# Moving the second half of a cross-attention value projection from the attention to behind the expert queries, with merge gates in quarter slots

## The reference, cut to what matters

```
h = rmsnorm(x)
ya = moba_attention(...)              # 8 heads
yb = nsa_attention(...)               # 8 heads: compressed, selected and window branch
g = sigmoid(h @ w_merge_gate + b_merge)          # 2 x 1024 columns
merged = g[:, :, 0] * (ya @ w_up_a) + g[:, :, 1] * (yb @ w_up_b)
x = x + merged @ w_out
x = x + peer_ffn(rmsnorm(x), ...)     # expert queries, key scores, top 16, experts u and v
for layer in (0, 1):
    ...
    kv = mem @ xa_wkv[layer]          # keys and values of the memory: do not depend on x
    x = layer_norm(alpha * x + cross_attend(x, kv, ...))
    ...
```

## Time and profile before

| | |
|---|---|
| median of 3 runs | 1773.57 us (1771.17 to 1774.9) |
| profiled execution, its own time from first to last instruction | 1771.5 us |
| its mean granted TensorE clock | 0.995 |
| TensorE busy | 1735.8 us, 98% |
| VectorE busy | 1119.2 us, 63% |
| ScalarE busy | 240.8 us, 14% |
| GpSimd busy | 301.4 us, 17% |
| DMA moved | 439.62 MB, mean 248 GB/s |

### The profile page before, as it was taken

One profiled execution on the slowest core, in us unless ns is written; L12 is line 12 of the kernel. 1 busy time (PEld: TensorE's weight loads), 2 busy tenths in 40 slices (PEclk: granted clock), 3 DMA queues, 4 the chain that ended last, 5 costly groups with the idle time before them and its releaser, 6 DMA issues.

```text
span 1771.5 us, 29553 instructions
## 1 busy us (share of the span) xinstructions
PE 1735.8 (98%) x11793; PEld 1482.8 (84%) x11793; DVE 1119.2 (63%) x2415; ACT 240.8 (14%) x599; POOL 301.4 (17%) x282
## 2 busy tenths in 40 slices
PE   8999999999999899999999999999999999999996
PEld 7898576986999899999999868699955978699942
DVE  4752432898657888799533533279974763379964
ACT  1014520110414111000000011111100001011100
POOL 0010000145433444444422200000000000000000
PEclk9999999999999999999999999999999999999998
DMA  7534234499999999999999844365554435354551
GB/s 276 190 122 164 72 119 143 155 337 372 414 416 416 405 407 398 373 412 415 415 417 418 344 202 160 126 223 172 171 173 166 167 121 191 117 170 167 170 182 50
DMA packets 76609, 439.62 MB, mean 248 GB/s; under 512 B 8566, under 2 KB 8656, under 8 KB 37840
## 3 DMA queue, kind: packets, MB, share of 16 engines
q1 hardware_dynamic: 42624, 305.15, 46.4%
q0 software_dynamic: 32592, 125.92, 18.3%
q10 hardware_dynamic: 1280, 6.95, 1.0%
HBM read 432.67 MB, written 5.24 MB: 247 GB/s over the span
## 4 chain that ended last, share of the span: by engine, by line
PE 81%; DMA 9%; DVE 8%; issue 1%; ACT 1%; POOL 0%; SPq 0%; POOLq 0%; DVEq 0%
PE ps L1139 16%; PE ps L921 14%; PE ps L540 10%; DMA arena<-u_rows,sparse_pairs 7%; PE ps L584 7%; PE ps L913 7%; PE ps L1177 4%; PE ps L623 3%; PE ps L498 3%; DVE arena L1912 2%; PE ps L776 2%; PE ps L823 2%; PE ps L789 1%; PE ps L934 1%; PE ps L1008 1%
## 5 line engine op out<-in xcount | busy, mean ns | idle before, releaser
L913 PE MATMUL ps<-xT,ring 128*128 128x150 f32 x2048 | 268.4, 293 | 0.0
L921 PE MATMUL ps<-arena,ring 128*128 128x150 f32 (+1 forms) x2048 | 266.3, 292 | 0.8 <-DMA ring<-stream 0.8
L913 PEld LDWEIGHTS ps<-xT,ring 128*128 128x128 f32 x2048 | 264.4, 191 | 0.1
L921 PEld LDWEIGHTS ps<-arena,ring 128*128 128x128 f32 x2048 | 262.3, 190 | 1.5 <-issue 1.5
L540 PE MATMUL ps<-ring,arena 128*128 128x512 f32 x416 | 181.4, 592 | 0.4 <-ACT arena L1487 0.4
L2033 DVE SCALAR_TENSOR_TENSOR arena<-arena,sparse_dots 128x1024 f32<-128x1024 f32 x105 | 134.7, 1283 | 73.4 <-DMA arena<-v_rows,sparse_pairs 68.2
L2501 POOL DMA_INDIRECT arena<-v_rows,sparse_pairs x107 | 132.8, 1241 | 224.9 <-DVE arena L2033 180.4
L1912 DVE CUSTOM_DVE_ANT_0 arena<-arena 128x1024 f32<-128x1024 f32 x107 | 127.9, 1223 | 66.9 <-DMA arena<-u_rows,sparse_pairs 66.3
L2501 POOL DMA_INDIRECT arena<-u_rows,sparse_pairs x107 | 132.4, 1238 | 167.9 <-DVE sparse_dots L1912 143.7
L2464 POOL TENSOR_SCALAR stat<-stat 128x1 f32<-128x1 f32 (+2 forms) x23 | 4.4, 190 | 913.8 <-DVE stat L2205 705.7
L540 PEld LDWEIGHTS ps<-ring,arena 128*128 128x128 f32 x416 | 78.0, 190 | 93.0 <-issue 92.3
(11 more groups left out here) (341 smaller groups left out, 2244.2 us busy)
## 6 DMA issues: line engine op xcount, KB each, us to landing
ring<-stream SPq DMA_DIRECT2D x288, 1024.0 KB, 7.5
arena<-second_params POOLq DMA_DIRECT2D x6, 1024.0 KB, 5.2
arena<-kv_scratch POOLq DMA_DIRECT2D x2, 2048.0 KB, 14.2
kv_scratch<-arena ACTq DMA_DIRECT2D x2, 1024.0 KB, 10.7
arena<-held_params ACTq DMA_DIRECT2D x1, 2048.0 KB, 16.5
arena<-u_rows,sparse_pairs POOLq DMA_INDIRECT x107, 13.7
arena<-v_rows,sparse_pairs POOLq DMA_INDIRECT x107, 11.2
arena<-second_params POOLq DMA_DIRECT2D x1, 1536.0 KB, 6.5
```

The lines of the kernel that those rows point to most:

```text
L913: ins = pe.matmul(ps[:, o % 2, 0:DENSE], w[:, (o % 2) * D + k * P:(o % 2) * D + (k + 1) * P], xT[:, k, 0:DENSE], start=(k == 0), stop=(k = ...
L921: ins = pe.matmul(ps[:, 4 + k // 2, c:c + DENSE], w[:, (o % 2) * D + k * P:(o % 2) * D + (k + 1) * P], H[:, n, :], start=False, stop=last, ...
```

## The change

In the attention, the merge gates are spread over all 16 units (4 products of 256 columns a unit, a quarter of a slot; a gate after units 3, 7, 11 and 15), and the section `v0` leaves it. `v0` now stands behind `peer_q` and ahead of `k1`, in the same form as `v1` (`memory_values`). Its stage in SBUF moves to the place of the upper expert queries, its spill moves from POOL's queue to ScalarE's, and ScalarE's wait for the spills stands after 8 turns of the expert loop and not after 12. The first memory spill keeps its place. The waits for the old spill on ScalarE, VectorE and POOL go away.

```
-            ("v0", 4), ("merge", 4), ("w_out", 4), ("peer_q", 8), ("k1", 4), ("v1", 4),
+            ("merge", 4), ("w_out", 4), ("peer_q", 8), ("v0", 4), ("k1", 4), ("v1", 4),
...
+        v0_stage = pqT[:, 8:16].rearrange("p j t -> p (j t)").rearrange("p (i n) -> p i n", i=TT)
...
             def fill(n):
 
-                if n < 8:
-                    s, t = n // 2, n % 2
-                    if t == 0:
-                        if s:
-                            pe.wait_ge(mgate_ready, 4 + s)
-                        fill_slots["gate"] = slot("mgate_b", s)
...
-                half, i, kh = (n - 8) // 4, n // 2 % 2, n % 2
...
-                for k in range(4):
-                    ins = pe.matmul(ps[:, 6, :], memT[:, 4 * kh + k, i * P:(i + 1) * P],
-                                    fill_slots[kh][:, k * 512:(k + 1) * 512],
-                                    start=(kh == 0 and k == 0), stop=(kh == 1 and k == 3))
...
+                s, t, kh = n // 4, n // 2 % 2, n % 2
+                if t == 0 and kh == 0:
+                    if s:
+                        pe.wait_ge(mgate_ready, 4 + s)
+                    fill_slots["gate"] = slot("mgate_b", s)
+                w = fill_slots["gate"]
+                for k in range(4 * kh, 4 * kh + 4):
+                    ins = pe.matmul(ps[:, 6, t * T:(t + 1) * T], w[:, k * 2 * P + t * P:k * 2 * P + (t + 1) * P],
+                                    xT[:, k, :], start=(k == 0), stop=(k == KT - 1))
+                if t == 1 and kh == 1:
                     ins.then_inc(slot_done, 1)
...
+            memory_values("v0", K0_FIRST)
             for c in range(4):
-                if c >= 2:
-                    pe.wait_ge(xkv_ready, KV_EARLY + c - 1)
+                pe.wait_ge(xkv_ready, KV_EARLY + c - 1)
                 feature_major(slot("k1", c), 4 + c % 2, memT).then_inc(slot_done, 1)
...
             def fill_copy(n):
 
-                if n % 2 == 0:
-                    return
-                if n < 8:
-                    merge_gate(4 + n // 2, START["mgate_b"] + n // 2 + 1, 6)
-                    return
...
-                act.copy(v0_stage[:, i, half * 512:(half + 1) * 512], ps[:, 6, :]).then_inc(xkv_ready, 1)
+                if n % 4 == 3:
+                    merge_gate(4 + n // 4, START["mgate_b"] + n // 4 + 1, 6)
...
-            act.wait_ge(kv_spilled, 32)
...
+            values_out("v0", v0_stage, 0)
+            act.wait_ge(xkv_ready, KV_EARLY)
+            act.dma_start(kv_scratch[0][:, KT * T:], v0_stage.rearrange("p i n -> p (i n)")).then_inc(v0_spilled, 16)
+            gate_exponentials(0)
...
-            at = 12
+            at = 8
...
+            act.wait_ge(v0_spilled, 16)
             act.wait_ge(kv1_spilled, 32)
...
-            dve.wait_ge(kv_spilled, 32)
...
-            pool.dma_start(kv_scratch[0][:, HALF_KV:], kv_stage[:, HALF_KV:]).then_inc(kv_spilled, 16)
```

More of the change, by code:

```diff
@@ L877, in _, with memory_values @@
             key_scores(PH + 3)
+            def memory_values(section, before):
+                for half in range(2):
+                    slots = [slot(section, 2 * half + kh) for kh in range(2)]
+                    for i in range(TT):
+                        if half or before > KV_EARLY:
+                            pe.wait_ge(xkv_ready, before + 2 * half + i - 1)
+                        for kh in range(2):
+                            for k in range(4):
+                                ins = pe.matmul(ps[:, 4 + i, :], memT[:, 4 * kh + k, i * P:(i + 1) * P],
+                                                slots[kh][:, k * 512:(k + 1) * 512],
+                                                start=(kh == 0 and k == 0), stop=(kh == 1 and k == 3))
+                            if i == 1:
+                                ins.then_inc(slot_done, 1)
+                        if i == 0:
+                            ins.then_inc(v_psum, 1)
+            memory_values("v0", K0_FIRST)
             for c in range(4):
[L879 to L880 removed]
+                pe.wait_ge(xkv_ready, KV_EARLY + c - 1)
                 feature_major(slot("k1", c), 4 + c % 2, memT).then_inc(slot_done, 1)
[L882 to L894 removed]
+            memory_values("v1", KV_EARLY + 4)
             for c in range(4 - K0_FIRST):
@@ L1393, in spill_second, with values_out @@
                 act.dma_start(kv_scratch[1][:, (n - 2) * KT * T:(n - 1) * KT * T], source).then_inc(kv1_spilled, 16)
+            def values_out(section, stage, done):
+                for half in range(2):
+                    for i in range(TT):
+                        if i == 0:
+                            act.wait_ge(v_psum, done + half + 1)
+                        else:
+                            act.wait_ge(slot_done, START[section] + 2 * half + 2)
+                        act.copy(stage[:, i, half * 512:(half + 1) * 512], ps[:, 4 + i, :]).then_inc(xkv_ready, 1)
+            values_out("v0", v0_stage, 0)
+            act.wait_ge(xkv_ready, KV_EARLY)
+            act.dma_start(kv_scratch[0][:, KT * T:], v0_stage.rearrange("p i n -> p (i n)")).then_inc(v0_spilled, 16)
+            gate_exponentials(0)
             for c in range(4):
@@ L1398, in _ @@
                     .then_inc(xkv_ready, 1)
-            gate_exponentials(0)
             spill_second(2, yT.rearrange("p k t -> p (k t)"))
-            for half in range(2):
-                for i in range(TT):
-                    if i == 0:
-                        act.wait_ge(v_psum, 2 + half + 1)
-                    else:
-                        act.wait_ge(slot_done, START["v1"] + 2 * half + 2)
-                    act.copy(v1_stage[:, i, half * 512:(half + 1) * 512], ps[:, 4 + i, :]).then_inc(xkv_ready, 1)
+            values_out("v1", v1_stage, 2)
             spill_second(3, mT.rearrange("p k t -> p (k t)"))
@@ L2473, in _ @@
             row_inverse(0)
-            HALF_KV = KT * T
             pool.wait_ge(xkv_ready, K0_FIRST)
@@ L2550, in _ @@
             pool.wait_ge(k0b_spilled, 16)
+            pool.wait_ge(v0_spilled, 16)
             def load_ln(n):
```

48 lines of the change are left out of this document (3 added, 45 removed).

## The result

| | kernel before | changed kernel |
|---|---|---|
| median | 1772.40 us (1771.17 to 1774.9, 4 runs) | 1782.16 us (1781.55 to 1783.52, 4 runs) |
| span of the profiled execution | 1771.5 us | 1780.5 us |
| mean granted TensorE clock in it | 0.995 | 0.994 |

The ratio is 1.0053, 95% interval 1.0041 to 1.0066: the change makes the kernel slower, by 9.8 us in the medians. The forecast was 1779.6 us, 6.0 us above the 1773.57 us of the first three runs of the kernel before; a fourth has moved that median to 1772.40. So the absolute time lies 2.6 us above the forecast, and the step from before to after 3.8 us above it: that the first is the smaller is luck with the base.

The account below looks back on a forecast made before the run. TensorE, busy 98% of a 1771.5 us span, was taken to bound the kernel. 27.5 - 13.0 - 1.6 - 6.9 = +6.0 us on the median of 1773.57 gave 1779.6 us, range 1774.5 to 1783.5.

Parts of the forecast that it names:

- Part 1: Behind the queries: the moved `v0` products add 27.5 us to TensorE, with nothing to hide them.
- Part 2: Attention, moba half: halved fills save 14.6 us, waits for gates in units 4 and 8 take 1.6, leaving 13.0 us.
- Part 3: Attention, nsa half: 5.8 us from thinner fills less 4.2 us for two new gates gives back only 1.6 us.
- The loop: Nsa half: a VectorE, TensorE, ScalarE cycle without fill sets the pace, two units taking 13.35 us instead of 14.81.
- Rival "the clock falls in the attention": Attention: TensorE's clock falls at the hole behind the last gate, costing 2.3 us, total 1781.9 us; chance 0.10.
- Part 4: Expert part: TensorE's wait for the second pair of one-hots goes, giving back 6.9 us including the lowered clock.
- Part 5: Elsewhere: moved spill, earlier spill wait, dropped waits and `v0` streaming beside row fetches cost nothing.
- The Trainium skill's drain: Nsa gates: the skill adds some 1.38 us per table switch, 2.8 us for two gates; the forecast left it out.
- The sum: Whole kernel: 27.5 - 13.0 - 1.6 - 6.9 = +6.0 us.
- the bounds of 10 and 24: Start of `merge`: forecast 14.6 us earlier; prediction wrong if less than 10 or more than 24 us earlier.
- The single waits: Attention: about 1 us for VectorE's scaling, over 2 us for unit 12's copy, near 3 us behind the last gate.
- The chances given beside the rivals: Whole kernel: 0.60 forecast, 0.22 cheap gates, 0.08 TensorE-limited attention, 0.10 clock fall, 0.02 stall remains; classes faster, within 0.2%, slower.

Follow-up runs that it names:

- e2: Changed kernel with the four attention gates computed by the exponential, no sigmoid and so no table switch, output differs: 1776.31 us, ratio 1.0013.
- e7: Kernel before, first half of `v0` kept as fill of the nsa units, second half moved behind the queries, gates untouched: 1776.6 us, ratio 1.0014.
- e4: Changed kernel with 23 useless products (10.6 us) in the nsa units, most per unit behind the gates of units 11 and 15: 1779.97 us, ratio 1.0036.
- e3: Changed kernel with one useless product of 256 columns in each nsa unit, 3.7 us in all: 1784.32 us, ratio 1.0054.
- e8: Changed kernel again, unedited: 1782.42 us, ratio 1.0062, profiled span 1778.4 us.
- e10: Changed kernel with two row dots fewer ahead of the second pair of one-hots: 1780.91 us, ratio 1.0051.
- e1: Changed kernel with the merge gates in the moba units alone and no fill in the nsa units: 1801.64 us, ratio 1.0156.
- e5: Kernel before with two constants altered, so two row dots fewer ahead of the second pair of one-hots: 1767.81 us, ratio 0.9966.
- e6: Kernel before with two of the four `k1` slots multiplied twice, 13.8 us of useless work behind the queries: 1781.58 us, ratio 1.0046.
- e9: Kernel before again, unedited: one execution of 1774.26 us, span 1772.5 us.

## Why the prediction was right in its sign, and what it mis-sized

**Part 1, `v0` adds 27.5 us.** 27.47 us. Right.

**Part 2, the moba half gives back 13.0 us.** The waits for gates are 1.06 and 0.43 us, for 1.0 and 0.6. The half gave 13.04 us, and the wait in unit 8 stands behind the mark: about 12.6 for 13.0 us. e2, without waits for gates, gives 40.72 - 26.55 = 14.2 us, for the 14.6 of the forecast's fills. Right within 0.4 us. One label was wrong: 177.77 us is where the fill of unit 7 starts, and not its scores, which start at 177.13. The sum used it as the start of the fill, so nothing changes.

**Part 3, the nsa half gives back only 1.6 us.** Right that it gives almost nothing, and by its mechanism. The loop was priced at 13.35 us a pair, and takes 13.57 us in the changed kernel. The pieces are those of the forecast but for one, the handover to the transposes in unit 13. VectorE's scaling ends there at 210.97, and TensorE, which had to wait with the values until 209.32, takes them to the end before it turns to the transposes (timelines of VectorE and TensorE, changed kernel):

```profile
210.10 0.87 DVE L1780 TENSOR_SCALAR arena<-arena 128x128 f32<-128x128 f32 x4
...
209.32 0.46 PE L749 MATMUL ps<-arena 128*128 128x128 f32 x2 [0.62 <-DVE arena L1787]
209.71 1.58 PE L754 MATMUL ps<-arena 128*64 128x128 f32 x16
211.22 0.66 PE L726 MATMUL ps<-small,arena 128*128 128x128 f32 x4
```

That is 0.25 us for the 0.05 us that I had put there. Measured without a switch, the half gave back 4.0 us (e2) and 4.2 us (e7), not 5.8. The table of stretches in e7 shows what is short there. Of the 1.6 us, 0.84 are a fall of the clock in units 9 and 10 (14.20 us, for 13.36 in e4, which has none there; the window from 190 to 200 us of e7 shows 0.83). Another 0.5 us are the two full pairs (13.66 and 13.57 us for 13.35). The rest, some 0.3 us, is that only two of my four pairs are full ones: units 9 and 10 took 14.06 us before and not 14.81, which left 0.75 us less to win there, and unit 8 and the tail together gave 1.97 us, 0.5 us more than a pair. In e2 the same stretch of units 9 and 10 has its fall (0.87 from 180 to 190 us). The two switches cost 3.7 us (63.02 - 59.34, the wait in unit 8 and a second fall of the clock among them); set against e7, which has no gate at all in this half, the gates cost 3.9 us (63.02 - 59.08), for the 4.2 + 0.6 of the forecast. In unit 12 the wait grew from 0.45 to 2.22 us, and ScalarE had no slack: its exponentials ended at 196.05 and the load began at 196.06 us.

**Rival "the clock falls in the attention"** had 0.10 and stood for one fall of 2.3 us. It came, smaller and twice: 1.2 us together. The first comes at the scores of unit 10 (182.32), with no gate since unit 7. The holes ahead of it are short (the timeline of the changed kernel):

```profile
179.40 0.66 PE L743 MATMUL ps<-arena 128*64 128x128 f32 x8 [0.62 <-DVE arena L1787]
181.11 0.66 PE L726 MATMUL ps<-small,arena 128*128 128x128 f32 x4 [1.04 <-DVE arena L1780]
```

So it wasn't the one long hole that I had looked for; that one, 2.61 us at 228.16, cost no clock (1.00 from 210 us to the end of the attention). The second fall does stand behind a long hole, the 2.22 us ahead of the scores of unit 12. It is there in the four profiles that have this hole (the changed kernel, e3, e8, e10), and missing in e2, e4 and e7, where the wait is 0.79, 0.49 and 0.54 us. The clock of e1 fell again and again: 0.50 from 188 to 212 us, 1.00 from 214 to 216, 0.50 from 218 to 220, 1.00 from 222 to 224, 0.50 from 226 to 236, with no hole over 2.35 us. The Trainium skill (TensorE: Matmul & The Clock Gate, "HAM oscillation") tells of idle gaps between bursts that return the array to half rate again and again. The trace of e1 agrees in kind. My chance for the rival rested on the length of one hole, and that was not enough to look at.

**Part 4, the stall gives back 6.9 us.** Right, by e5 (6.7 us), e6 and e10; in the execution of e9 the stall was 7.9 us long. VectorE's reserve ahead of the second one-hots was forecast as 28.3 - 14 = 14 us; its last instruction for them starts at 584.42 and takes 1.22 us, and TensorE comes at 599.06: 13.4 us.

**Part 5, nothing elsewhere.** No new wait in the expert part, and none for the spills.

**The Trainium skill's drain** (ScalarE: Activation LUTs, "What ACT_TABLE_LOAD costs"): the load of unit 11 starts 0.01 us behind the end of the exponentials' last instruction, takes 1.28 us, and the sigmoids start 0.02 us behind it. There is no drain of 1.38 us in this trace, and here the measurement decides.

**The sum.** In the undisturbed profile of e8 the terms are 27.47 - 13.04 - 0.39 - 6.87 = +7.2 us, with 1778.4 - 1771.5 = 6.9 us between the spans; forecast was +6.0. The term that is mis-sized is the attention's: 13.4 us given back and not 14.6. Without switches (e2) it gives 14.2 + 4.0 = 18.2 us for a forecast of 20.4, and the gates take 4.7 us of it for 5.8, the changed kernel's two falls of the clock among them (in e2 one). `merge` starts 245.68 - 232.19 = 13.5 us earlier there and 11.6 in the first profile, for 14.6, both inside the bounds of 10 and 24; the first expert block 14.0 and 15.9 us later, for 12.9. The single waits came as they were named: about 1 us for VectorE's scaling, 2.22 us for the copy in unit 12, 2.61 us behind the last gate. The medians differ by 9.8 and 9.5 us, more than that profile. For the rest there are only the clocks listed with the executions. The eight of the changed kernel have a granted clock of 0.991 to 0.996 (mean 0.9936) and take 1779.74 to 1785.09 us, the slower the lower. The 39 of the kernel before that stand beside e1 to e10 have 0.993 to 0.996 (mean 0.9947) and take 1770.48 to 1777.64 us, again the slower at the lower clock. (0.9947 - 0.9936) x 1780 = 2.0 us, an estimate, since each clock has three digits. Falls that come with some executions, as the early one with its 1.7 us, are by this a little more frequent or deeper in the changed kernel; where all of them lie, two profiles of each kernel don't show, and it stays open.

The chances given beside the rivals add up to 1.02, and those by class (0.09, 0.23, 0.68) to 1.00: the two sets don't fit together to the last hundredth.

One more step was wrong, without effect on the number: I set the span of 1771.5 us against the median as the execution's own time. A span of 1780.5 us belongs to a time of 1782.29 us, one of 1772.5 to 1774.26: 1.8 us lie around the span (1.7 to 2.1 in all executions on record). The profiled execution was no faster than the others.

## What to carry to other kernels

Before moving fill work out of a pipeline, add up the loop that holds no fill: the fill is free for as long as the loop is the longer, and past that point moving it costs its full length elsewhere. Here the moba half gave nearly all of its time back (13.0 of 14.6 us), since TensorE set its pace, and the nsa half gave 0.3 us for 13 us of fill taken out.

An engine that waits for a late partner can be served by making the partner earlier; look for the constant that orders its queue before moving products. Two row dots gave 6.7 us, and a change that removed the same stall as a side effect cost more than it gained.

Behind a change that thins TensorE's work, read the granted clock in windows of a few microseconds over the whole stretch, and not only at the longest hole.

## What the runs showed of the hardware that I had not expected

- The nsa half without fill, TensorE busy 56 to 73%, ran 20 us at a granted clock of 0.50 and then at 0.61 to 0.67, and took 69.76 us where the same work with 27.5 us of products in it took 63.30 (e1, before). A low busy share is not enough to tell it: in the next 10 us of e1 TensorE is busy 54%, and the clock is 1.00.

```profile
240.00:250.00 10.00, 5.39 (x46) 4.15 (x44) 6.45 (x35) 4.74 (x17) 0.00 (x0) 1.00 0.00 0
```

- 10.6 us of useless products in the same half kept the clock at 1.00, and the kernel was no slower for them (e4). 3.7 us of them did away with the fall at unit 10 alone (e3).
- The clock also fell with TensorE busy all the time: from 90 to 94 us to 0.55 and 0.60 in the changed kernel, behind 32 products of 24 columns, and at nearly the same place in four profiles of twelve, at some 1.7 us each. The other eight have the same products there and no fall. What sets it off in one execution and not in another, the traces don't show.
- The length of a hole did not tell whether the clock falls. Holes of 2.61 and 1.33 us at the attention's end brought no fall in either profile of the changed kernel nor in e10, and a fall to 0.50 in e3. Holes of at most 1.04 us ahead of the scores of unit 10 brought one in these three profiles, in e2 and in e7.
